# A two-block transformer kernel whose weight, gated and attended tiles start at other offsets within 128 bytes

## The reference, cut to what matters

```python
h = h + y @ w_out[l]
h = h + swiglu(rmsnorm(h, g_ffn[l]), w_gate[l], w_up[l], w_down[l])
...
return _merge_blocks(o) @ w_out
...
u = x @ w_in
...
return (jax.nn.silu(g) * val) @ w_out
```

## Time and profile before

| | |
|---|---|
| runs | 1810.24, 1810.76, 1812.06 us; median 1810.76 |
| profiled execution | 1809.7 us, its span from first to last instruction 1807.9 us |
| instructions | 26,859, of them 8,755 matmuls |
| TensorE busy | 1762.5 us, 97% of the span, mean granted clock 0.995 |
| GpSimd busy | 1032.6 us, 57% |
| ScalarE, VectorE busy | 796.2 us (44%), 765.0 us (42%) |
| memory read | 152.15 MB, 85 GB/s over the span |

### The profile page before, as it was taken

One profiled execution on the slowest core, in us unless ns is written; L12 is line 12 of the kernel. 1 busy time (PEld: TensorE's weight loads), 2 busy tenths in 40 slices (PEclk: granted clock), 3 DMA queues, 4 the chain that ended last, 5 costly groups with the idle time before them and its releaser, 6 DMA issues.

```text
span 1807.9 us, 26859 instructions
## 1 busy us (share of the span) xinstructions
PE 1762.5 (97%) x8755; PEld 1476.5 (82%) x8755; DVE 765.0 (42%) x1382; ACT 796.2 (44%) x1674; POOL 1032.6 (57%) x926
## 2 busy tenths in 40 slices
PE   8999999999999999999999999999999999999997
PEld 6879888888887888788888888877777888888887
DVE  7963000002235556553333322487875533333224
ACT  5644323322245555464444422555565644444231
POOL 7966555555562333466666655655554666666651
PEclk9999999999999999999999999999999999999999
DMA  4312333323334454323333233233322233332332
GB/s 154 92 47 83 104 93 93 97 87 108 91 99 106 126 134 117 87 82 98 100 93 93 87 105 94 76 94 82 86 76 76 66 110 98 93 100 83 105 91 98
DMA packets 327252, 171.94 MB, mean 95 GB/s; under 512 B 43458, under 2 KB 316948, under 8 KB 327188
## 3 DMA queue, kind: packets, MB, share of 16 engines
q1 hardware_dynamic: 327172, 171.12, 33.7%
q10 hardware_dynamic: 16, 0.00, 0.0%
HBM read 152.15 MB, written 2.10 MB: 85 GB/s over the span
## 4 chain that ended last, share of the span: by engine, by line
PE 85%; DVE 9%; ACT 2%; issue 1%; POOL 1%; DMA 1%; SPq 0%; DVEq 0%; ACTq 0%
PE bank L963 23%; PE bank L965 23%; PE bank L964 23%; DVE score L2246 3%; PE attended L963 2%; PE attended L965 2%; PE attended L964 2%; PE turned L1404 1%; PE attended L1420 1%; PE bank L1036 1%; PE bank L1048 1%; DVE small L2434 1%; ACT pmap L1841 1%; PE bank L1049 0%; DMA raw<-in_a_w_in 0%
## 5 line engine op out<-in xcount | busy, mean ns | idle before, releaser
L722 POOL TENSOR_TENSOR WL<-raw,WH 128x512 fp32r<-128x512 f32 (+3 forms) x656 | 778.0, 1208 | 542.0 <-ACT WH L1585 539.7
L963 PE MATMUL bank<-XL,WH 128*128 128x512 f32 x1432 | 568.9, 397 | 3.7 <-DVE work L2557 1.2
L965 PE MATMUL bank<-XH,WL 128*128 128x512 f32 x1432 | 557.8, 390 | 0.0
L964 PE MATMUL bank<-XH,WH 128*128 128x512 f32 x1432 | 557.1, 389 | 0.0
L1585 ACT ACTIVATE WH<-raw 128x512 fp32r<-128x512 f32 (+3 forms) x656 | 338.4, 566 | 298.0 <-PE bank L965 177.9
L965 PEld LDWEIGHTS bank<-XH,WL 128*128 128x128 f32 x1432 | 269.4, 188 | 57.0
L963 PEld LDWEIGHTS bank<-XL,WH 128*128 128x128 f32 x1432 | 269.9, 188 | 55.9 <-DVE work L2557 1.5
L964 PEld LDWEIGHTS bank<-XH,WH 128*128 128x128 f32 x1432 | 270.1, 189 | 50.2
L963 PE MATMUL bank<-HL,WH 128*128 128x512 f32 (+1 forms) x528 | 198.6, 376 | 0.0
L965 PE MATMUL bank<-HH,WL 128*128 128x512 f32 (+1 forms) x528 | 198.4, 376 | 0.0
L964 PE MATMUL bank<-HH,WH 128*128 128x512 f32 (+1 forms) x528 | 198.4, 376 | 0.0
(11 more groups left out here) (366 smaller groups left out, 2523.1 us busy)
## 6 DMA issues: line engine op xcount, KB each, us to landing
raw<-in_ffn_w_in SPq DMA_DIRECT2D x88, 512.0 KB, 3.7
raw<-in_w_gate SPq DMA_DIRECT2D x22, 512.0 KB, 3.7
raw<-in_w_up SPq DMA_DIRECT2D x22, 512.0 KB, 3.7
raw<-in_ffn_w_out SPq DMA_DIRECT2D x28, 384.0 KB, 3.2
raw<-in_ffn_w_out SPq DMA_DIRECT2D x28, 320.0 KB, 3.1
raw<-in_a_w_in SPq DMA_DIRECT2D x16, 512.0 KB, 3.9
raw<-in_kv_w SPq DMA_DIRECT2D x32, 256.0 KB, 2.9
raw<-in_w_in SPq DMA_DIRECT2D x12, 512.0 KB, 3.8
```

Of the source, the lines that this page charges most:

```text
L722: pool.tensor_tensor(wl, x, wh, ALU.subtract).then_inc(w_lo, 1)
L963: pe.matmul(out_, wh, xl, start=start, stop=False)
L964: pe.matmul(out_, wh, xh, start=False, stop=False)
L965: return pe.matmul(out_, wl, xh, start=False, stop=stop)
```

## The change

Four unused buffers are added; nothing else. 16 floats (64 bytes) stand ahead of `WH`, so that `WH`, `WL` and `par` start at 64 modulo 128 bytes; 16 floats behind `par` bring `ones` and all behind it back to 0. Within the FFN's stack 16 floats put `HH`, `HL`, `act_g`, `hid` at 64. Within attention's stack 8 floats (32 bytes) put `OH`, `OL`, `OF`, `pmap` and all of the heads' operands at 32; `PTH` and `PTL`, ahead of them, stay at 0. `XH`, `XL`, `raw`, `xres`, `yout` keep their addresses; what lies behind `par` moves up by 128 bytes.

```diff
         raw = sb("raw", [P, RAW, DT, P])
+        sb("ahead_of_weights", [P, 16])
         WH = sb("WH", [P, SLOTS, DT, P], F32R)
         WL = sb("WL", [P, SLOTS, DT, P], F32R)
         par = sb("par", [P, 6 * P])
+        sb("behind_parameters", [P, 16])
         ones = sb("ones", [P, P])
...
         ffn = ExitStack()
+        sb("ahead_of_hidden", [P, 16], stack=ffn)
         HH = sb("HH", [P, FT, S], F32R, stack=ffn)
         HL = sb("HL", [P, FT, S], F32R, stack=ffn)
...
         PTL = sb("PTL", [P, 2, QT * KEYS + S - P], F32R, stack=att)
+        sb("ahead_of_attended", [P, 8], stack=att)
         OH = sb("OH", [P, DT, S], F32R, stack=att)
```

## The result

The changed kernel takes 1842.33 us (median of 4 runs, 1840.65 to 1843.06), the kernel before beside it 1811.41 us (4 runs, 1810.24 to 1813.4). The ratio is 1.0168, 95% interval 1.0151 to 1.0186: slower by 31 us. The forecast was no change, 1796 to 1830 us.

What follows compares the result with a forecast made beforehand. TensorE, busy 97% of the span, was taken as the bound. With no instruction changed and every duration term taken as 0, the sum was 0 and the forecast 1810.8 us, no change (0.62), range 1796 to 1830 us.

Steps and rivals of the forecast that it cites:

- the first rival: Long streams of X products: 64 bytes between weights and moving operand sets the gates' slower rhythm; 17.3 us, 1828 us; chance 0.13.
- A distance of 64 bytes costs nothing there. Value taken: 0: Weights at 64, norm's output at 0, 4440 matmuls of 512 columns: change 0, ends +5.1 and -2.6 ns each.
- the reading of the gates: The 16 gates' stretch, 231.7 ns: triples with weights at 0 and at 64 equally slow, so distance 64 was called free.
- the distance between the operands stays 0: Gated tiles and weights both at 64: value 0, ends -1.3 and +1.3 ns on 1386 + 396 matmuls, 2.3 us.
- whether a start as such matters: Gated tiles' term: the convolution's off-line starts, 119.3 ns against 118.8 in down0, taken to show no dependence.
- the second rival: Weight and moving-operand reads meet less at 64 bytes: -11.5 us, 1799.3 us, outer bound 1762; faster had chance 0.20.
- third rival: Attended tiles and heads at 32 lose 5 ns each: 2.4 + 4 us = 6.4 us, 1817 us; chance 0.05.
- the 11 ns beyond streaming: Length-independent part of a 512-column matmul, beside 215.6 ns of streaming; an address could touch it, 49 us if all went.
- its weakest step: Taking the gates' 16-column loads and the convolution's 256-column stream as short stand-ins for 4440 matmuls with full loads.
- two classes: POOL: operands a multiple of 32 bytes apart are slower (1.29 us against 1.04); all distances stay multiples, so no duration changes.
- The rule of the Trainium skill on 16-byte lines: SBUF is read in 16-byte lines and crossing one pays; offsets 32 and 64 are whole lines, so the sum is 0.
- The rule of the Trainium skill on transfers: Packing of heads' operands: descriptors off 256-byte multiples fetch extra bytes, 2.3 us becoming at most 2.5 us, hidden.

Runs made afterwards that it cites:

- e11: Kernel before plus a measurement behind its last output: six starts, varied load widths and streamed lengths; 226.67 ns at 0 with 128 loaded, 512 streamed; no whole time given.
- e12: Kernel before with one 64-byte pad ahead of the norm's output, all distances as before: 1810.84 us against 1811.25, ratio 0.9996.
- e2: Kernel before with only the two stack pads: gated tiles at 64, attended tiles and heads at 32, weights at 0; 1813.96 us, ratio 1.0023.
- e1: Kernel before with only the two pads around the weights, so weights and parameters at 64, the rest at 0; 1836.32 us, ratio 1.015.
- e14: Kernel before with both weight buffers 16 bytes further, all moving tiles at distance 240; median 1839.75 us, ratio 1.0152.
- e10: Kernel before plus a measurement behind its last output: 64 starts, 0 to 252 bytes, 512 columns; paces 226.67 to 240.0 ns, about 560 us added.
- e18: Kernel before with the weight buffers shifted so all moving tiles are at distance 156; median 1830.99 us, ratio 1.0133.

## Why the prediction was wrong

Right were the bound (TensorE, at one pace for each length), that no other engine's operation would change (busy times within 3 us), that POOL, ACT, VectorE and the packing would add no wait to speak of, and the place of the loss in the first rival: the long streams of X products. It was given 0.13 and 17.3 us. The gu stages lost 20.1 us: the step is 6.67 ns and not 5.1, on 3024 matmuls; the other 360 of its 3384 stand in the first 150 us, where most of the loss is hidden.

The step that failed is "A distance of 64 bytes costs nothing there. Value taken: 0", and the reading of the gates under it. As a stand-in they do not serve. They load 16 columns, and e11 shows that loads of 32 columns sit near 231 ns at every distance, 0 included (231.67 ns at 0 and at 64, the same as the gates' 231.7; 16 columns were not measured by themselves). So the triples at 0 were as slow as those at 64 not because 64 is free, but because 0 has lost its advantage. Under full loads the change's distance, 192, costs 6.67 ns a matmul, where 0 was taken. In the changed kernel the gates have not moved from 231.7 ns: (546.50 - 541.17)/23 in its timeline:

```profile
541.17 0.39 PE L967 MATMUL attended<-XL,PTH 128*16 128x512 f32 x1
...
546.50 0.39 PE L969 MATMUL attended<-XH,PTL 128*16 128x512 f32 x1
```

The second step that failed is "the distance between the operands stays 0" for the gated tiles. It does modulo 128; modulo 256 it becomes 128, and the down stages lost 8.7 us where the text allowed 2.3. I had written down the addresses modulo 256 for three buffers and used them for transfers alone.

The convolution was another stand-in, for "whether a start as such matters". It was right on its own question (e12: moving all starts by 64 bytes does nothing), and was then used against the second rival and beside the gates for the long streams, of which it is no witness: it streams 256 columns, and there e11 has no slow distance at all, 116.7 to 118.7 ns against 120.0 at 0. Its 119.3 ns against 118.8 said nothing on 512. The 118.8 was itself too low, read from eight distances: over the 90 distances shown above the pace is 120.0 ns, so that 512 columns are 213.3 ns and 13.3 are left that do not depend on the length, not 11.

The attended tiles and heads (third rival) moved to 96 modulo 256 from the weights. Attention with its out stages lost 4.3 us of 33.3, less than the 6.4 that was allowed, but products with the norm's output stand in it too, and e2, which moves these tiles without the weights (distance 32), lost nothing there (-0.3 us). Whether the third rival holds stays open.

The second rival, that something in the 11 ns beyond streaming is a conflict that a distance could lessen, has its half: it is the distance between load and stream that counts, and for 256 columns a distance does lessen it, 113.3 ns in e1 against 120.0. But 226.67 ns is the least that any of some hundred streams of 512 columns settled at; there the distance 0 was already at the best.

What made the sum 0 in the end was to rest it on short, odd streams when the term was 4440 matmuls of one shape. The text named this as its weakest step and gave the slower time 0.18 in all.

For POOL the prediction had two classes, operands "a multiple of 32 apart" and not. At 4 bytes the split became faster, but at 16 it did not (1.31 us, e14), so that the rule is wrong; it cost nothing here, since the change's distances were all multiples of 32.

The rule of the Trainium skill on 16-byte lines ("SBUF — State Buffer", "SBUF: two separate sides"), read as the prediction read it, that 32 and 64 cost nothing, is not borne out here: at 512 columns distances of whole lines cost from 0 (240 bytes in e10) to 8 ns a matmul (208 bytes), and starts within one line differ by up to 13 ns (240 and 244 bytes). The rule of the Trainium skill on transfers ("DMA: Bandwidth & Descriptors", "How a descriptor splits into AXI transactions") could have cost only what is hidden, and the packing still lands in a median of 2.3 us.

What stays open: what in the memory or in the engine makes these rhythms. The runs show that the shapes of load and stream matter, that at the multiples of 32 bytes and 512 columns the paces follow the difference of the two starts modulo 256 bytes whatever the starts are, and that for other distances more than one rhythm is stable. For 256 columns two kernels at 64 differ, and no run says why. Nor do the runs show which reads meet where.

## What to carry to other kernels

Where TensorE is the bound, look at the distance between starts in its long streams to a tenth of a nanosecond, and, where the streams are of 512 columns under full loads in float32r, keep the moving tile and the weights at the same start modulo 256 bytes. Here every kernel with another distance was slower by 0.2 to 2%, and the loss shows in no wait, only in the count of matmuls in a window. For other shapes measure: with 256 streamed columns the same start was among the slowest. An added small buffer between the two, if its size is not a multiple of 256 bytes, is enough to lose it. A stand-in from the same trace has to have the same shape in both operands before it says anything on a term with thousands of members.

## What the runs showed of the hardware that I had not expected

The settled paces of 512 columns are few: 226.67, 228.89, 230.0 and 233.33 ns come again and again, in stages and in the measurements behind the end, with some others up to 240.0, and at the multiples of 32 bytes the stages repeat them to 0.1 ns from kernel to kernel. 226.67, 233.33 and 240.0 are 34, 35 and 36 times 6.667 ns, and the 113.33 and 120.0 of 256 columns are 17 and 18 times. A kernel can hold 226.67 ns over one whole stage and 233.33 over the next like one at the same addresses (e14, e18). Narrower loads (64 and 32 columns) do not make a stream of 512 columns faster but slower, 230.0 and 231.67 ns against 226.67 at equal starts.
